# GLA decay exponents as matrix products and 64x64 score tiles, MLA values stationary, in a hybrid encoder step

## The reference

```
def gla_chunk(S, q, k, v, la):
    b = jnp.cumsum(la, axis=2)
    dec = jnp.exp(jnp.where(incl, b[:, :, :, None, :] - b[:, :, None, :, :], -jnp.inf))
    att = jnp.einsum('bhid,bhjd,bhijd->bhij', q, k, dec)
    o = jnp.einsum('bhij,bhjv->bhiv', att, v) + jnp.einsum('bhid,bhdv->bhiv', q * jnp.exp(b), S)
    S_new = jnp.exp(b_last)[..., None] * S + jnp.einsum('bhjd,bhjv->bhdv', k * jnp.exp(b_last - b), v)

# MLA, one block of queries of one head
    p = jax.nn.softmax(jnp.where(mask, s * scale, -jnp.inf), axis=-1)
    return jnp.einsum('bhqk,bkhd->bqhd', p, v)
```

## Time and profile before

| what | us |
|---|---|
| runs of the kernel before (median, lowest to highest of 3) | 2626.19 (2612.37 to 2630.95) |
| the profiled execution, its own time | 2631.12 |
| its span on the core | 2629.3 |
| phase_gla | 382.3 to 503.1, so 120.8 |
| phase_mla_attend | 1618.0 to 1843.4, so 225.4 |
| phase_out(2) | 1843.4 to about 1925 |

### The profile page before, as it was taken

One profiled execution on the slowest core, in us unless ns is written; L12 is line 12 of the kernel. 1 busy time (PEld: TensorE's weight loads), 2 busy tenths in 40 slices (PEclk: granted clock), 3 DMA queues, 4 the chain that ended last, 5 costly groups with the idle time before them and its releaser, 6 DMA issues. The chain is left out here.

```text
span 2629.3 us, 32574 instructions
## 1 busy us (share of the span) xinstructions
PE 2175.1 (83%) x12836; PEld 1822.5 (69%) x12836; DVE 1648.5 (63%) x1851; ACT 1295.7 (49%) x1421; POOL 261.2 (10%) x326
## 2 busy tenths in 40 slices
PE   2689769897584799999999087999957999999990
PEld 1689758797484688888887054666846888888870
DVE  0354118644455688888898323544456889888883
ACT  1235511122312677777776242333125777777772
POOL 0122120041000111111100000000001110111100
PEclk6789885698795899999999588988858999999995
DMA  8277440000222699999999504000326999999974
GB/s 322 76 254 257 172 150 1 5 1 5 84 91 95 244 363 371 373 373 385 372 366 321 193 12 155 1 1 1 123 103 243 374 368 366 369 361 371 370 286 162
DMA packets 160168, 561.27 MB, mean 213 GB/s; under 512 B 34012, under 2 KB 40056, under 8 KB 126864
## 3 DMA queue, kind: packets, MB, share of 16 engines
q1 hardware_dynamic: 138064, 538.85, 55.4%
q0 software_dynamic: 21952, 20.32, 2.3%
HBM read 557.65 MB, written 50.70 MB: 231 GB/s over the span
## 5 line engine op out<-in xcount | busy, mean ns | idle before, releaser
L1888 DVE TENSOR_TENSOR ex_wl<-ring,ex_wh 128x2048 fp32r<-128x2048 f32 x384 | 867.9, 2289 | 113.0 <-ACT ex_wh L1843 113.0
L1843 ACT CAST ex_wh<-ring 128x2048 fp32r<-128x2048 f32 x384 | 712.4, 1910 | 0.0
L226 PE MATMUL ex_p<-ex_wh,ex_xh 128*128 128x512 f32 x1024 | 414.7, 405 | 8.3 <-DVE ex_xl L1893 8.3
L226 PE MATMUL ex_p<-ex_wl,ex_xh 128*128 128x512 f32 x1024 | 402.8, 393 | 0.0
L226 PE MATMUL ex_p<-ex_wh,ex_xl 128*128 128x512 f32 x1024 | 402.3, 393 | 0.0
L226 PEld LDWEIGHTS ex_p<-ex_wh,ex_xh 128*128 128x128 f32 x1024 | 194.7, 190 | 46.2 <-DVE ex_xl L1893 9.9
L226 PEld LDWEIGHTS ex_p<-ex_wl,ex_xh 128*128 128x128 f32 x1024 | 194.2, 190 | 42.5
L226 PEld LDWEIGHTS ex_p<-ex_wh,ex_xl 128*128 128x128 f32 x1024 | 194.9, 190 | 36.8
L226 PE MATMUL ex_py<-ex_wh,ex_gh 128*128 128x512 f32 x512 | 200.2, 391 | 2.8 <-DVE ex_gl L1909 2.8
L226 PE MATMUL ex_py<-ex_wl,ex_gh 128*128 128x512 f32 x512 | 200.4, 391 | 0.0
L226 PE MATMUL ex_py<-ex_wh,ex_gl 128*128 128x512 f32 x512 | 200.0, 391 | 0.0
(11 more groups left out here) (397 smaller groups left out, 4045.9 us busy)
## 6 DMA issues: line engine op xcount, KB each, us to landing
ring<-in_moe_w SPq DMA_DIRECT2D x384, 1024.0 KB, 7.2
ring<-in_ada_w SPq DMA_DIRECT2D x24, 2048.0 KB, 12.1
ring<-in_ab_w_in SPq DMA_DIRECT2D x7, 2048.0 KB, 9.8
mod<-mod SPq DMA_DIRECT2D x16, 512.0 KB, 7.5
cb_y<-yrow SPq DMA_DIRECT2D x16, 512.0 KB, 9.8
xres<-x SPq DMA_DIRECT2D x12, 512.0 KB, 3.7
x<-xres SPq DMA_DIRECT2D x12, 512.0 KB, 9.5
ring<-in_ab_w_out SPq DMA_DIRECT2D x2, 2048.0 KB, 11.7
```

Source lines behind the costliest of these rows:

```text
L226: ins = nc.tensor.matmul(out, a, b, start=first and n + m == 0, stop=last and n == len(terms) - 1 and m == 2)
L1843: nc.scalar.copy(part(wh, u), g.view(base + u)).then_inc(hi_ready, 1)
L1888: nc.vector.tensor_tensor(part(wl, u), g.view(base + u), part(wh, u).bitcast(F32), ALU.subtract).then_inc(lo_ready, 1)
```

## The change

In phase_ab_project the low-rank product gives la token-major, in five products, with the bias as one more row of the weight; no division and no scan remain. In phase_gla the exponents of all levels, of the running sum and of the distance to the tile's end become products of la with constant 0/(1/16) matrices (`K_DC`, `K_SUF`) in PSUM, from where ACT takes the exponential. The scores of each level are made only where the level has any: six levels and the diagonal as 64x64 tiles on the two diagonal blocks, each in its own quarter of the array, and the last level as one 64x64 tile off the diagonal. DVE masks 7x64 columns for two heads at a time and sums by a tree of additions; ACT copies the off-diagonal block. The output products both use 128 rows (decayed q padded with zeros). In phase_mla_attend the probabilities are scaled before they are transposed (`normalise`), ACT copies the transposed blocks of a whole head into a row, and the values of a head are made once a head with the values stationary (64 columns) and up to 512 tokens moving, which gives the output feature-major; ACT and DVE take its high and low parts for two heads at a time. phase_out(2) gets these parts and neither transposes nor splits.

The core of the diff (phase_gla's TensorE and DVE, MLA's TensorE, phase_ab_project's DVE):

```diff
-                ch(nc.vector.scalar_tensor_tensor(laz[:], laz[:], 0.0, lae[:], ALU.min, ALU.subtract))
-                for j in range(2):
-                    nc.vector.tensor_scalar(a.b2[:, 0:4, j, :], laz[:, j, 0:SEQ].rearrange("p (t n) -> p t n", n=P), 1.0 / 16.0, None, ALU.mult)
-                    ch(nc.vector.tensor_scalar(a.b2[:, 4, j, 0:DSEQ], laz[:, j, SEQ:TOK], 1.0 / 16.0, None, ALU.mult))
-                for t in range(NT):
-                    for j in range(2):
-                        ch(nc.vector.tensor_tensor_scan(lae[:, 0, 0:P], g.c(K_ONE, P), a.b2[:, t, j, :], 0.0, ALU.mult, ALU.add))
-                        ch(nc.vector.tensor_copy(a.b2[:, t, j, :], lae[:, 0, 0:P]))
+                ch(nc.vector.scalar_tensor_tensor(a.la[:], laz[:], 0.0, lae[:], ALU.min, ALU.subtract))
+                ch(nc.vector.memset(a.la[32:64, NT - 1, :], 0.0))
+                ch(nc.vector.memset(a.la[64:P, NT - 1, :], 0.0))
...
+                def exponents(t):
+                    for j in range(2):
+                        if 2 * t + j:
+                            pe.wait_ge(e_ready, 2 * t + j)
+                        for n in range(2):
+                            last = nc.tensor.matmul(pe_x[:, 4 * n:4 * n + 4, :], a.la[:, t, j * P:(j + 1) * P], g.c(K_DC + 512 * n, 512),
+                                                    start=True, stop=True)
+                        last.then_inc(x_done, 1)
...
+                    for l in range(LEV - 1):
+                        for c, h in ((0, hs[0]), (1, hs[1]), (1, hs[0]), (0, hs[1])):
+                            m = em[rows(h), t % 2, l, at_col(c)]
+                            nc.tensor.matmul(ps[blk(c), h, l, :], m, m, start=True, stop=True)
...
+                for t in range(NT):
+                    for pair in range(2):
+                        scores(t, pair)
+                    states(t)
+                    if t + 2 < NT:
+                        exponents(t + 2)
+                    if t:
+                        outputs(t - 1)
+                outputs(NT - 1)
...
+                    dve.wait_ge(mk_ready, 2 * t + 2)
+                    ch(nc.vector.tensor_tensor(mk[:, :, 0:3, :], mk[:, :, 0:3, :], mk[:, :, 3:6, :], ALU.add))
+                    ch(nc.vector.tensor_tensor(mk[:, :, 0, :], mk[:, :, 0, :], mk[:, :, 1, :], ALU.add))
+                    ch(nc.vector.tensor_tensor(mk[:, :, 2, :], mk[:, :, 2, :], mk[:, :, 6, :], ALU.add))
+                    dve.wait_ge(far_ready, t + 1)
+                    for c in range(2):
+                        r = slice(HB * c, HB * c + HB)
+                        ins = nc.vector.tensor_tensor(at[r, t % 2, :, r], mk[r, :, 0, :], mk[r, :, 2, :], ALU.add)
+                    ins.then_inc(at_ready, 1)
+                    if t + 1 < NT:
+                        decayed(t + 1)
...
+                    for j in range(NT - 1):
+                        nc.tensor.matmul(po[at, 0, j * P:SEQ], m.v[:, j, c:c + MV], pT[:, b, row(j):row(j + 1)],
+                                         start=j == 0, stop=j == NT - 2)
...
                 for i in range(steps):
                     h, t = divmod(i, NT)
-                    if i + 1 < steps:
-                        scores(i + 1)
+                    if i + 2 < steps:
+                        scores(i + 2)
                     if t == 0 and h % 2 and h + 1 < MH:
                         keys_of((h + 1) // 2)
-                    if t == 2 and h + 1 < MH:
+                    if t == 1 and h + 1 < MH:
                         queries_of(h + 1)
                     transposes(i)
-                    if i:
-                        values(i - 1)
-                values(steps - 1)
+                    if t == 1 and h:
+                        values(h - 1)
+                values(MH - 1)
```

More of the change, by code:

```diff
@@ L690, in _ @@
                 pe.wait_ge(fm_free, 5)
-                pe.wait_ge(par_here, 96)
-                for j in range(2):
-                    halves(5 + j, P, lambda out, tok: nc.tensor.matmul(out, wal[:, j * P:(j + 1) * P], lrT[0:GLR, tok], start=True, stop=True))
+                pe.wait_ge(wal_here, 32)
+                for i in range(3):
+                    pe.wait_ge(fm_free, 5 + i - 1)
+                    for t in range(2 * i, min(2 * i + 2, NT)):
+                        w = width(t)
+                        last = nc.tensor.matmul(z[0:w, (5 + i) % 2, t % 2, 0:256], lrT[:, t * P:t * P + w], wal[:], start=True, stop=True)
+                    last.then_inc(fm_done, 1)
                 pe.wait_ge(mod_sum, 2)
@@ L1551, in _ @@
                         tok = slice(t * P, t * P + w)
[L1552 removed]
+                        if u == 0 and gated:
                             if t + 1 < NT:
@@ L2292, in phase_mla_attend @@
 @phase
-def phase_mla_attend(g, m, o):
+def phase_mla_attend(g, m, oh, ol):
     nc, io = g.nc, g.io
@@ L2301, in phase_mla_attend @@
         rope = sb("rope", [P, TOK])
-        turned = sb("turned", [P, 2, TOK])
+        turned = sb("turned", [P, TOK])
         qT = sb("qT", [QM, 2, TOK])
-        p = sb("p", [P, 2, SEQ])
-        pT = sb("pT", [P, 2, NT - 1, P])
+        p = sb("p", [P, 3, SEQ])
+        pT = sb("pT", [P, 2, sum(SEQ - P * j for j in range(NT - 1))])
+        pTs = sb("pTs", [P, 2, 2, DSEQ])
         nm, sm = sb("nm", [P, steps]), sb("sm", [P, steps])
@@ L2319, in phase_mla_attend @@
         cut = lambda j: key_cols(j).stop - key_cols(j).start
+        row = lambda j: sum(SEQ - P * i for i in range(j))
         with nc.Block() as block:
```

469 lines of the change are left out of this document (260 added, 209 removed).

## The result

The changed kernel takes 2521.88 us (median of four runs, 2520.04 to 2530.38) against 2624.27 us before in the same session: the ratio is 0.9621, with a 95% interval of 0.9579 to 0.9663. The direction and most places were right; the size was not.

The account below looks back on a forecast made before the run. DVE and PE share phase_gla's bound; PE bounds phase_ab_project and phase_mla_attend. Terms: -45 (phase_gla) - 0.5 (phase_ab_project) - 3 (phase_mla_attend) - 6 (phase_out(2)) = -54.5, taking 2626.2 to 2572 us; range 2545 to 2611.

Parts of the forecast that it names:

- VectorE's chain of 7.1 us from scores to scores: phase_gla: masks and sums of 3.6 us, the next tile's decay of 3.2 and three handovers give 7.1 a tile.
- Which clock: phase_gla: at a clock of 0.8, a quarter of the way from 69 to 92 us, 75 us, so -45.
- s = 4: phase_gla: a tile's 120 score instructions were taken to last 4 us, with bounds 3.2 and 12.8.
- my fast end, 69: phase_gla: the whole phase at 2.4 GHz, 49 + 5 s = 69 us, a gain of 51.
- my 15 and 24: phase_gla: the start before the first scores, 15 us at 2.4 GHz or 24 at 1.2; before, it took 10.
- the sign: phase_mla_attend: heads without keys lasting 10.7 to 11.2 us would show the forecast right; before, 11.5.
- the waits for the keys' copy: phase_mla_attend: the next head's queries wait for DVE's two copies, 0.8 seven times, a loss of 5.6 us.
- 0.6 a head: phase_mla_attend: idle time of 0.73 and 0.19 mostly goes with exponentials two steps ahead, -9.6 us in all.
- rival (2): phase_mla_attend: MLA's clock falls from 0.88 to 0.80, +20 us, kernel 2595; chance 0.17.
- phase_ab_project: -0.5 forecast: phase_ab_project: scans and divisions leave DVE, but PE is busy throughout; -0.5 us, ends -2 and +2.
- phase_out(2): -6 forecast: phase_out(2): first product no longer behind transposed, split input, -3.4 us; three more transposition groups go, about 2.6.
- the rivals: Chances: phase_gla stays at 1.2 GHz 0.20; MLA's clock falls 0.17; small tiles collide 0.07; phase_gla's DVE chain too long 0.08.

## Why the prediction was right and wrong

In this pair of profiles the kernel gained 111 us, 57 more than forecast: 17 more in the attention, 17 in the norms, 8 in phase_gla, and 15 in phases with small terms or none. The step that failed is TensorE's clock. I left it at its mean in the attention, took a mixture in phase_gla, and gave it no term elsewhere.

*phase_gla: 75 us forecast, 68.5 measured, -52.6 instead of -45.* The mechanism held. VectorE's chain of 7.1 us from scores to scores was 7.5 in the first tile (397.16 to 404.71). Two terms were mis-sized. "Which clock": I went a quarter of the way from the fast to the slow case, by the 0.69 and 0.91 of two later stretches; the first four tiles ran at 1.00. And the score time: s = 4, with its bounds worked out at 1.2 GHz, went unchanged into the sum at 2.4. It fits the fifth tile, at 1.2 GHz (3.6), but the four before it took 2.0 each, since all four quarters work at once and at 2.4 GHz (0.017 an instruction; 0.107 at 1.2 GHz is 0.053 alone at 2.4, and a quarter of that is 0.013). That my fast end, 69, meets the measured time is therefore luck: with s = 2 it would be 59. The missing 9 are the start (17.7, from 377.44 to 395.14, between my 15 and 24), the tiles (one wait of 0.82 for the outputs (414.23), a buffer that the outputs still read, makes the second tile 10.4 instead of 9.6, and the third too) and the last tile, which starts at the low clock (10.9 instead of 7.9).

*phase_mla_attend: -3 forecast, -20 measured.* The terms that I listed add up to -2.7, and to -5.9 with the 0.2 a head that the values were to gain, so -3 leaves that out. Some single terms were about right: a head without keys lasts 10.85 (1640.47 to 1651.32, queries to queries) where I named 10.7 to 11.2 as the sign, and the waits for the keys' copy are 7.7, of which 1.8 at the start stood there before too: 5.9 where I had 5.6. In sum they came to nothing, since PE waits 19.7 us before and 19.6 after. The step that failed is that I priced the removed waits at their own length only, 0.6 a head, at an unchanged clock. The clock of this phase rose from 0.88 to 0.97, and that is the whole gain: PE's 212.1 us of work at 0.88 would be 212.1 x 0.88/0.97 = 192 at 0.97, and 191.2 was measured. That it rose because the waits left the turns is the reading above, not shown by a run that changes this alone. I had weighed the clock only as a loss, in rival (2), for the half-filled columns; full weights of 128 columns changed nothing at 0.97, so that reason was empty.

*phase_ab_project: -0.5 forecast, -4 measured* (294.1 to 290.1, from its first product). That product itself comes 0.9 us earlier (87.33 for 88.20), since two transfers ahead of it were moved behind; a dip of the clock near 300 us was 3.4 us shorter in the changed kernel. Not tested apart.

*phase_out(2): -6 forecast, -6.3 measured.* The first product came when the first low part was ready, 4.3 us after the phase's start.

*What was in no term:* the two norms, -8.9 and -8.1 in the pair of profiles; the gdn phases behind phase_gla, -4.6, which begin at a higher clock; the first experts with what follows, -4.0, whose cause was not looked for. In the medians the norms may count for less, since kernels with the old code up to the first norm show both lengths; the runs of the kernel before lie between 2612.37 and 2630.95.

Of the rivals none occurred. Outside phase_gla the clock made about 20 us in the attention and, in this pair of profiles, 17 in the norms, and I had let it count there as a risk only; the 4.6 in the gdn phases go with it too, which no run shows apart. The range was too narrow below for the same reason: its lower end held the attention at 0.93. Fine stretches of the earlier trace rows would have shown beforehand that nine of the ten falls of the clock sit behind the waits that the change removes.

## What to carry to other kernels

Before pricing a removed wait by its length, look in fine stretches where the granted clock falls: where the falls sit behind that wait, carry a case in which the slow stretches go with it, and expect another wait moved there to bring some of them back, as the keys made earlier did (8.5 of 20 us). Use a price at the clock of the case that it goes into: here one price stood in both. Scores that need only part of a tile are worth cutting to quarters of the array: four 64x64 instructions took 0.067 us, where one alone would take 0.053 by the estimate above. And where an order gains by working further ahead, check that each thing behind it is ready too; the old value products, two steps ahead, only met their wait elsewhere, and the kernel lost 36 us.

## What was unexpected of the hardware

TensorE at 92% busy with 64-row products fell from 1.00, and the mean of the next 101 us was 0.52, while a phase that waits for VectorE in every tile (1.88, 0.94 and 0.95 us), with quarter-array and full-array products in turn, held 1.00 until its fourth tile. Two attentions in which PE waits 19.7 and 19.6 us in all ran at 0.88 and at 0.97. The same norm, with the same instructions at the same distances, took 26 or 35 us by the clock alone, and full-array work placed ahead of it did not settle which.
